# A load queue's order: four output-projection chunks of a linear attention ahead of the last eight modulation chunks, the first key chunk ahead of two, and one modulation sum after a layer norm

## The reference, cut to what matters

```python
# GLA: h (272, 1024) -> mix (272, 1024)
q, k, v, r, z = split(h @ gla_w_in)                 # widths 512, 512, 1024, 1024, 16
log_g = log_sigmoid(z @ gla_w_gate_up + b) / 16
o = chunked_linear_attention(q, k, v, log_g)        # four heads, chunks of 64 tokens
o = normalize(o) * norm_g                           # per head
mix = (o * silu(r)) @ gla_w_out                     # (1024, 1024)
h = layer_norm(ALPHA * h + mix)                     # "ln2" in the kernel
h = layer_norm(ALPHA * h + experts(h))
...
# second block
mod = silu(c) @ w_ada + b_ada                       # (1024) @ (1024, 6144): six groups of 1024
```

## Time and profile before

| | us |
|---|---|
| median of 3 runs | 2074.46 (2073.27 to 2078.7) |
| the profiled execution's own time | 2075.74 |
| its span, first to last instruction | 2074.0 |
| PE busy | 1847.6 (89%) |
| DVE busy | 621.1 (30%) |
| ACT busy | 487.8 (24%) |
| DMA, mean over the span | 281 GB/s |

### The profile page before, as it was taken

One profiled execution on the slowest core, in us unless ns is written; L12 is line 12 of the kernel. 1 busy time (PEld: TensorE's weight loads), 2 busy tenths in 40 slices (PEclk: granted clock), 3 DMA queues, 4 the chain that ended last, 5 costly groups with the idle time before them and its releaser, 6 DMA issues.

```text
span 2074.0 us, 29038 instructions
## 1 busy us (share of the span) xinstructions
PE 1847.6 (89%) x12173; PEld 1086.7 (52%) x12173; DVE 621.1 (30%) x1267; ACT 487.8 (24%) x831; POOL 351.5 (17%) x306
## 2 busy tenths in 40 slices
PE   8998999989947699999999999999985866599996
PEld 7977999757925333333333333333324856444442
DVE  6776554356354400000000000000006655401102
ACT  5844434224312100000000100000004443321120
POOL 3000000000000599999800000000001000000000
PEclk9998999988978799999999999999996976789998
DMA  6446565447422999999999999999975420569994
GB/s 197 148 130 223 183 204 192 154 134 247 139 82 102 359 410 403 420 413 410 403 419 414 411 403 413 416 411 409 409 294 166 141 81 1 203 250 419 419 420 196
DMA packets 185007, 583.04 MB, mean 281 GB/s; under 512 B 11161, under 2 KB 77354, under 8 KB 158240
## 3 DMA queue, kind: packets, MB, share of 16 engines
q1 hardware_dynamic: 182256, 575.09, 72.1%
q0 software_dynamic: 2608, 5.97, 1.1%
HBM read 579.96 MB, written 1.05 MB: 280 GB/s over the span
## 4 chain that ended last, share of the span: by engine, by line
PE 70%; DMA 14%; DVE 10%; ACT 4%; issue 2%; SPq 1%; DVEq 0%; ACTq 0%
PE ps L1725 17%; PE ps L440 8%; PE ps L442 8%; PE ps L441 8%; DMA ring<-in_moe_w_out 7%; PE ps L2160 6%; PE ps L1730 5%; PE ps L1761 4%; DMA ring<-in_moe_w_in 3%; PE ps L2184 3%; DVE wlo L473 2%; PE ps L1766 1%; ACT whi L465 1%; DMA raw<-in_gla_w_in 1%; PE ps L2145 1%
## 5 line engine op out<-in xcount | busy, mean ns | idle before, releaser
L1725 PE MATMUL ps<-ring,xg 128*64 128x512 f32 x1624 | 411.9, 602 | 13.0 <-ACT sgm L1835 5.8
L473 DVE TENSOR_TENSOR wlo<-raw,whi 128x2048 fp32r<-128x2048 f32 (+6 forms) x97 | 213.8, 2209 | 243.1 <-ACT whi L465 242.8
L1725 PEld LDWEIGHTS ps<-ring,xg 128*64 128x64 f32 x1624 | 121.8, 137 | 219.9 <-issue 208.5
L465 ACT ACTIVATE whi<-raw 128x2048 fp32r<-128x2048 f32 (+6 forms) x97 | 178.7, 1844 | 229.1 <-PE ps L442 86.1
L440 PE MATMUL ps<-xh,whi 128*128 128x272 f32 (+1 forms) x712 | 212.9, 299 | 3.0 <-DVE xl L540 2.7
L1761 PE MATMUL ps<-ring,ahm 128*64 128x512 f32 x824 | 204.5, 597 | 11.4 <-DMA ring<-in_moe_w_out 10.4
L442 PE MATMUL ps<-xh,wlo 128*128 128x272 f32 (+1 forms) x712 | 210.4, 295 | 0.0
L441 PE MATMUL ps<-xl,whi 128*128 128x272 f32 (+1 forms) x712 | 210.0, 295 | 0.0
L2093 POOL TENSOR_SCALAR lnt<-lnt,h 128x384 f32<-128x384 f32 x120 | 188.6, 1572 | 12.2
L1899 DVE TENSOR_TENSOR sgm<-sgm,ps 128x512 f32<-128x512 f32 x28 | 18.2, 685 | 513.3 <-PE ps L1730 513.3
L727 POOL DMA_DIRECT2D lnt<-in_ln_gain x4 | 2.2, 561 | 856.8 <-issue 525.1
(11 more groups left out here) (568 smaller groups left out, 2489.0 us busy)
## 6 DMA issues: line engine op xcount, KB each, us to landing
ring<-in_moe_w_in SPq DMA_DIRECT2D x203, 1024.0 KB, 17.9
ring<-in_moe_w_out SPq DMA_DIRECT2D x103, 1024.0 KB, 19.9
ring<-in_w_gate SPq DMA_DIRECT2D x29, 1024.0 KB, 14.1
raw<-in_ffn_w_in SPq DMA_DIRECT2D x28, 1024.0 KB
ring<-in_w_down SPq DMA_DIRECT2D x26, 1024.0 KB, 13.4
raw<-in_w_ada SPq DMA_DIRECT2D x24, 1024.0 KB
more<-in_moe_w_in SPq DMA_DIRECT2D x21, 1024.0 KB, 18.1
ring<-in_w_up SPq DMA_DIRECT2D x20, 1024.0 KB, 11.5
```

Of the source, the lines that this page charges most:

```text
L465: e.activation(whi[0:rows, s % NSPL, 0:n], raw[0:rows, i % NRAW, 0:n], ACT.Copy).then_inc(S.hi.s, S.hi.up((s,)))
L473: e.tensor_tensor(wlo[0:rows, s % NSPL, 0:n], raw[0:rows, i % NRAW, 0:n], whi[0:rows, s % NSPL, 0:n].bitcast(F32), ALU.subtract).then_inc( ...
L1725: e.matmul(ps_[b][64 * v:64 * v + 64, :], a[:, kk_, 64 * v:64 * v + 64], both[v][:, k, 512 * b:512 * b + 512], start=kk_ == 0, stop=kk_ == 7)
```

## The change

The load list is put in another order at two places. `gk` 0 goes ahead of ada 10 and 11. The four `go` chunks go ahead of ada 16 to 23. In `dve_gla`, `dve_ada(e, 4)` goes behind layer norm "ln2". Nothing is added or removed, and PE's and ACT's own orders stay as they are (`for _ in range(2)` is the same loop).

```diff
     M.add(("gz", 0), 128, 128, by_rows(w_gl, 3072, 8, 16))
-    plan_ada(2)
     for j in range(2):
         M.add(("gk", j), 128, CW, by_rows(w_gl, 512 + 256 * j, 8, 256))
-    plan_ada(2)
+        plan_ada(2)
     for j in range(2):
         M.add(("gq", j), 128, CW, by_rows(w_gl, 256 * j, 8, 256))
     plan_ada(2)
...
     for j in range(4):
-        if j % 2 == 0:
-            plan_ada(2)
         M.add(("go", j), 128, CW, by_blocks(d["gla_w_out"][0], j, 128))
-    plan_ada(4)
+    plan_ada(8)
...
-        for j in range(2):
+        for _ in range(2):
             split_hi(e, M, s)
...
+        dve_ln_tiles(e, "ln2", (XTILES[:1], XTILES[1:]))
         dve_ada(e, 4)
-        dve_ln_tiles(e, "ln2", (XTILES[:1], XTILES[1:]))
```

## The result

The changed kernel takes 2051.94 us (median of 4 runs, 2051.01 to 2053.99), the kernel before 2074.69 beside it (4 runs, 2073.27 to 2078.7). The ratio is 0.9889, with a 95% interval of 0.9871 to 0.9906: 22.75 us or 1.1% faster. The prediction said 2050, with 2046 to 2056 as its range. Its profiled execution took 2052.08 us with a span of 2050.3, against 2075.74 and 2074.0 of before.

A forecast was written before the change was run, and what follows sets the result against it. The prediction took the chain of waits up to `perm`, for which the experts' weight stream waits, as the bound. 5.5 + 15.9 + 6.0 - 2.2 = 25.2 us off 2075.74 gave 2050, range 2046 to 2056.

The forecast's parts named there:

- A: First key chunk `gk` 0, ahead of turn x2: issued earlier, DVE's split loses its idle time; 5.5 us won.
- It can't be more: At `gk` 0: the gain is at most 5.5 us, as DVE has nothing idle left there.
- B: The four `go` chunks: issued earlier, the norm of the outputs starts at 584.65 instead of 600.50; 15.9 us won.
- C: Layer norm ln2: DVE's sums no longer wait behind PE's group 4 columns; 6.0 us won.
- The new wait: PE waits ahead of ada 19, whose slot `go` 3's split frees late; 2.2 us lost.
- A chunk alone takes 4.2 us: Transfer time of a lone chunk from issue, used to put ada 19's landing at 633.3.
- that wait: PE wants ada 17 at 586.0 and it lands at 586.6; 0.6 us, hidden under the norm.
- Rival 1: Clock falls in the wait for ada 19, costing up to 3.5 us: 21.7 us won, 2054; chance 0.17.
- Rival 2: ada 19, 20 and 21 share the engines: wait 8.2 us, gain 19.2, 2056; chance 0.12.
- Rivals 3, 4 and 5: Another wait holds DVE, 2064 us, 0.05; experts' stream sets end, 2075, 0.02; late ada 19 makes it slower, 0.02.
- The sum: Whole kernel: 5.5 + 15.9 + 6.0 - 2.2 = 25.2 us won, 2050.5 against the profiled 2075.74.

The follow-up runs named there:

- l_dve_only: Kernel before, load list untouched, with DVE's share of `go` 2 moved behind its part of turn x3: 2058.13 us, ratio 0.9907.
- c_ln: Kernel before with only DVE's modulation sum of group 4 moved behind layer norm ln2: 2068.8 us, ratio 0.9969.
- b_go: Kernel before with only the four `go` chunks moved ahead of ada 16 to 23: 2063.36 us, ratio 0.9936.
- d_one_ahead: Changed kernel with ada 16 moved ahead of `go` 3 in the load list: 2048.28 us, ratio 0.9862.
- g_alone: Changed kernel with ada 20 and all behind it issued only after PE has used ada 19: 2052.44 us, ratio 0.9882.
- h_warm: Changed kernel with 28 unused matmuls on PE between ada 18 and 19: 2050.68 us, ratio 0.9869.
- a_key: Kernel before with only `gk` 0 moved ahead of ada 10 and 11: 2069.22 us, ratio 0.9963.
- k_both: d_one_ahead with DVE's `go` 1 and 2 splits later, ada 16 before `go` 2, ada 17 before `go` 3, PE's ada 18 between x3's tiles: 2045.69 us.

## Why the prediction was right, and which term was off

**A, right** (5.5, measured 5.6). DVE's row at 453.49 follows line 662, without the 5.53 us. But 5.5 was worked out from the shortest of the four transfers seen here in the old order. "It can't be more" was wrong for that reason: against the others it is 6.7 to 7.0. PE did not wait for ada 10 and 11. Their 32 matmuls follow x2's products at once (3.64 us from 465.98 at a granted clock of 0.50, where before had 2.58 us from 471.20 at 0.74), and by ada 12 at 486.04 (491.73 before) the us that this cost was made up.

**B, right** (15.9, measured 16.0). DVE does both splits in one row, as predicted, and the norm starts 21.62 us earlier. `l_dve_only` shows the cause apart: it was DVE's order. The list was one of two ways to mend it, and the dearer one.

**C, right** (6.0, measured 6.0; 6.6 by the medians of `c_ln`).

**The new wait: right in place and cause, too small in size.** It was put at 2.2 us, ahead of ada 19 and with the slot of `go` 3 as its cause; `b_go` and `d_one_ahead` confirm both. It was 3.23. The step that failed is "A chunk alone takes 4.2 us". It took the middle of the window 438 to 439 of the earlier trace rows for the last bytes, which in windows of 0.2 us move until 438.7 (a share of 0.12 from 438.6 to 438.8, 0.01 behind), 4.4 us after the issue. And it left out what lies between the last bytes and PE. ada 19 was issued at 608.27 and PE started 5.35 us behind that. For ada 17 it was 5.4 us (576.79 to 582.21), and where the prediction gave that wait 0.6 us it was 1.70, hidden as foreseen. In `g_alone`, 0.6 us lie between the last bytes and PE. The Trainium skill, page "Perfetto Trace Analysis", section "DMA Instruction — HWDGE (DVE, Sync)", says that an engine's last descriptor updates the semaphore only after the write before it is confirmed; the 0.6 us agrees with that in kind, and no run here takes it apart.

**Rival 1 came true, at a smaller price.** The clock did fall in the wait, to 0.50. The forecast had put this at nothing and its chance at 0.17. That chance hung on the 2.2 us: at 3.2 the wait is as long as the idle time of the earlier trace rows that had made the clock fall. The price was 1.4 us (`h_warm`), not up to 3.5: it had been taken from seven us at half clock, and here the low clock lasted from 613.2 to 616.6, by the shares of the windows that hold its two ends (0.59 and 0.85).

**Rival 2 fell.** ada 20 and 21 cost ada 19 0.2 us at most. Rivals 3, 4 and 5 fell with B's 16.0 us and with the end, which followed `perm`.

**The sum.** In the prediction's terms 5.6 + 16.0 + 6.0 - 3.2 - 1.4 is 23.0 instead of 25.2, and the 0.8 us of `go` 0 and 1 and the net 0.1 of the first and the last row but one make it 22.1. That is 3.1 us short of the forecast. The profiled execution took 2052.08 us, only 1.6 above the 2050.5 of the sum, because the program behind `perm` happened to run 1.6 us shorter than in the trace of before. So part of the nearness is luck. The 0.8 isn't put down to the change: x3 begins at low clock in both kernels, and `c_ln`, whose code and order there are those of before, took 12.71 us for `go` 0 and 1, while `a_key` took 11.31. What sets the moment at which the clock comes back there stays open.

## What to carry to other kernels

A late transfer need not cost anything by itself: `go` 2 did because its first user stood ahead of urgent work in an engine's fixed order. So ask two questions of such a stall, whether the chunk can come earlier and whether its user can stand further back: moving one DVE step won 16.7 us with no transfer moved, and moving the transfers won 12.1. When the order of a ring of slots changes, write down for each chunk whose slot it gets and when that one is used up: three times here a gain on DVE came back in part as a wait that followed from the slots (3.23 us ahead of ada 19, 9.02 ahead of ada 17, 9.21 ahead of ada 18). And when two traces are compared, count from a point that neither change touches: the start of the stretch alone moved by up to 3 us between traces.

## What the runs showed of the hardware that was not expected

- A 1 MB modulation chunk issued by SP with nothing just ahead of it was in use by PE 5.1 to 5.5 us after its issue (609.27 to 614.41 alone in `g_alone`, 608.27 to 613.62 and 576.79 to 582.21 in the changed kernel), in `g_alone` 0.6 us after its last bytes. Two chunks issued right behind it cost it 0.2 us at most. A chunk issued 0.42 us ahead of it cost about 2: 7.28 us in `k_both` (586.06 to 593.34).
- One and the same transfer, `gk` 0 behind ada 11, took 9.03, 10.08, 10.26 and 10.38 us in four traces.
- A wait of PE of 3.0 to 3.2 us behind a run of matmuls at full clock let the granted clock fall from 1.00 to 0.50 (three kernels), the level of 1.2 GHz, and 16 matmuls took 1.94 instead of 1.07 us. A wait of 1.70 us (ahead of ada 17) left it at 1.00. With 3.61 us of spare matmuls in the wait it stayed at 1.00, and that won 1.4 us.
